# Ahead of the first four pairs of chunks: tiles of x turned as they land, low halves of a chunk in two parts, copies and sums of quanta in another order

## The chip, the cores and the metric

The kernel runs on one core of one Trainium2 chip. The metric is device time in microseconds (us) of one launch, from runs without a profile; the profile is of one further execution. A change of under 0.2% is about what a measurement of this kernel can't tell from none.

## The reference

Two blocks of a transformer in sequence, in float32, for 256 tokens of width 1024. The first block has two layers with adaptive norms over the tokens `x` and a context `ctx` of 256 more; the second has two layers with three attentions each. Only the start of the first layer matters here:

```python
m = jax.nn.silu(cond) @ w_ada + b_ada            # adaln_terms: shift, scale, gate
xl = rms_norm(h_lat, norm_w[li]) * (1.0 + scale_l[:, None, :]) + shift_l[:, None, :]
xc = rms_norm(h_ctx, norm_w[li]) * (1.0 + scale_c) + shift_c
...
au_l, av_l, az_l, bq_l, bk_l, bv_l, bz_l = jnp.split(xl @ w_in, EVEN_SPLITS, axis=-1)
```

Before any product of layer 0 can run, x must be turned so that its columns lie on partitions, its mean squares taken, and the product `silu(cond) @ w_ada` done for the columns concerned. `w_ada` is large: 24 quanta of 256 columns, 1 MB each, are used in the first layers.

## The kernel before

Five engines run hand-written lists of instructions that wait for each other by semaphores; nothing is reordered by a scheduler. Weights come in chunks of 512 KB, numbered r. SyncE (SP) issues their loads into `raw` (four buffers, `load_raw`, L757): the load of chunk r waits until `lo_done` counts r-3, so until chunk r-4 has been split. ScalarE (ACT) copies a chunk into `w_hi` (L839, `split_hi`), VectorE (DVE) writes the rest into `w_lo` (L1341, `split_lo`), and each product is three matmuls: hi x hi, lo x hi, hi x lo (L2088 to L2090).

The start is a pipeline over four pairs. A pair is two of the eight tiles of 128 columns of x, the chunk r = pair of the weights called `av`, and two quanta of `w_ada` (2 x pair and 2 x pair + 1). For each quantum TensorE (PE) multiplies it (`condition`, L2183, banks sc and ac in turn, half by half as the halves land), ACT copies the sum (`ada_evacuate`, L881), PE turns the copy (`condition_turn`, L2199), DVE finishes it (`ada_finish`, L1482 and L1483). With both quanta of a pair done DVE makes the factors (`modulation`, L1488) and the four norm tiles of the pair: `norm_tmp` (L1405) on DVE, `norm_hi` (L854) on ACT, `norm_lo` (L1415) on DVE. Then PE does the pair's products (`value_part`, two tiles e = 0, 1, four groups of 128 tokens n = 0 to 3, three matmuls each).

Ahead of it the four blocks of 128 tokens (two of x, two of ctx, 512 KB each) land in `x_tok`. DVE sums their squares. PE waits for the nine small vectors and for all four blocks, turns the vectors (L2234), and turns x tile by tile (`turn_x`, L2260, four transposes a tile, banks tr in turn), each tile copied into `x_t` by ACT (L860).

After the four pairs come the chunks `au` (r = 4 to 7, slots 4 to 7). Ahead of slot 6 stands `condition_pair(0)` (L2187, its matmuls are L2183 too): the sums of quanta 8 and 9, two halves each. The list of SP that feeds all this is fixed; behind the load of chunk 7 it issues twelve small loads (L788 to L800), then chunk 8, then the four halves of quanta 8 and 9 (L768):

```python
for r in range(HELD, RB + LAYERS_2 * C2):
    load_raw(r)
    ...
    if r - 2 in ADA_OF_SLOT:
        for n in ada_pair(ADA_OF_SLOT[r - 2]):
            load_ada(n)
    if r == 7:
        ...
```

Of the kernel before, what the change touches and what calls it, by code (L numbers as in the profile page):

```python
# [18 lines left out]
F32 = mybir.dt.float32  # L19
F32R = mybir.dt.float32r  # L20
I32 = mybir.dt.int32
ALU = mybir.AluOpType
# [148 lines left out]
NADA = 3 * KT  # L171
ADA_COLS = 256
ADA_FIRST, ADA_ALL, NADA_RAW = 8, 24, 4

# [239 lines left out]
def build_program(nc, t, out):  # L414

    with ExitStack() as ctx:
# [10 lines left out]
        with nc.sbuf_tensor("ada_raw", [P, NADA_RAW, KT, ADA_COLS], F32) as ada_raw:  # L427
# [110 lines left out]
            sem("misc_in"), sem("stored"))  # L538
        rows_in = sem("rows_in")
        ones_set, eps_set, lam_set = sem("ones_set"), sem("eps_set"), sem("lam_set")  # L540
# [100 lines left out]
        def source_at(r):  # L641

            if r >= RB:
# [10 lines left out]
                       (V_QN, t["c_q_norm_w"].rearrange("l (k p) -> (l k) p", p=P)),  # L654
                       (V_KVN, t["c_kv_norm_w"]))

        def ada_bank(n):
# [164 lines left out]
        def _(act):  # L822
# [77 lines left out]

            turned(0, vec[:], tr[:, 0, 0:V_END])
            act.wait_ge(tr_free, 1)
# [3 lines left out]
            def x_turned_to(k):  # L906
                use = TR1_OF[("x", k)]
                turned(use, x_t[:, k, :], tr[:, use % 2, :])

# [4 lines left out]

            for k in range(3):
                x_turned_to(k)
            ada_evacuate(0)
            x_turned_to(3)
            ada_evacuate(1)
            x_turned_to(4)  # L920
            split_hi(0)
            modulated_hi(0, 0)
            x_turned_to(5)
            x_turned_to(6)
            modulated_hi(0, 1)
            x_turned_to(7)
            for pair in range(1, 4):
                ada_evacuate(2 * pair)
                ada_evacuate(2 * pair + 1)
                split_hi(pair)  # L930
                modulated_hi(pair, 0)
                modulated_hi(pair, 1)
            nc.scalar.activation(small[:, 60:61], ones[:, 0:1], ACT.Gelu)
# [392 lines left out]
        def _(dve):  # L1326
# [8 lines left out]
            def split_lo(r):  # L1335
# [6 lines left out]
                last.then_inc(lo_done, 1)  # L1342

            rotations = [0]

# [147 lines left out]
            def modulated_norm(layer, v0, v1, chunk=None):  # L1493
                dve.wait_ge(rs_set, layer + 1)
                for v in range(v0, v1 + 1):
                    u = 2 * KT * layer + v
                    if v < v1:
                        k, half = norm_tile(layer, v)
                        norm_tmp(u, k, (LAT, CTX)[half], amod[:, layer, half, k:k + 1], (LAT, CTX)[half])
                    if chunk is not None and v == v0 + 1:  # L1500
                        split_lo(chunk)
                    if v > v0:
                        k, half = norm_tile(layer, v - 1)
                        norm_lo(u - 1, k, (LAT, CTX)[half], mod[:, layer, k, half:half + 1])

            norm_rsqrt(0, 4)
            for pair in range(4):
                ada_finish(2 * pair)
                if pair:
                    split_lo(pair)  # L1510
                ada_finish(2 * pair + 1)
                dve.wait_ge(ada_set, 2 * pair + 2)
                modulation(0, 2 * pair, 2 * pair + 2, 2 * pair + 2)
                modulated_norm(0, 4 * pair, 4 * pair + 4, chunk=None if pair else 0)
            split_lo(HELD)
# [563 lines left out]
        def _(pe):  # L2079
# [152 lines left out]
            pe.wait_ge(ident_in, 16)  # L2232
            pe.wait_ge(vec_in, 16 * 9)
            nc.tensor.transpose(tr[:, 0, 0:V_END], vec_rows[0:V_END, :], const[0:V_END, K_ID:K_ID + V_END]).then_inc(tr_done, 1)  # L2234
            pe.wait_ge(ones_set, 1)
            for n in range(4):
                pe.wait_ge(x_in[n], 16)
            def value_part(name, j, e, tiles=range(4)):
                c = L0_CHUNKS.index((name, j))
                k, (wh, wl) = 2 * j + e, split_views(c)  # L2240
                if e == 0:
                    pe.wait_ge(lo_done, c + 1)
                for n in tiles:
                    tok = slice(P * n, P * n + P)
                    if name == "av":
                        pe.wait_ge(n_lo, 2 * k + n // 2 + 1)
                    if k == 0 and n == 3:
                        pe.wait_ge(tr_free, TR1_OF[("x" if name == "av" else "ws", KT - 2 if name == "av" else 0)] + 1)
# [13 lines left out]

            turn_x(0)
            turn_x(1)
            turn_x(2)
            pe.wait_ge(cond_set, 1)
            condition(0)
            turn_x(3)
            spread(0, 4)
            condition_turn(0)  # L2270
            condition(1)
            turn_x(4)
            condition_turn(1)
            turn_x(5)
            turn_x(6)
            condition(2)
            turn_x(7)
            for pair in range(4):
                if 0 < pair < 3:
                    condition(2 * pair + 2)  # L2280
                value_part("av", pair, 0, (0, 1))
                if pair < 3:
                    condition_turn(2 * pair + 2)
                    condition(2 * pair + 3)
                value_part("av", pair, 0, (2, 3))
                if pair < 3:
                    condition_turn(2 * pair + 3)
                value_part("av", pair, 1)

# [454 lines left out]
```

## Time and profile before

| | us |
|---|---|
| median of 3 runs (1054.69 to 1056.17) | 1055.52 |
| the profiled execution's own time | 1054.3 |
| its span, first to last instruction | 1052.2 |
| PE busy | 1032.1 (98%) |
| DVE, ACT busy | 733.7, 591.1 |

The span is the profiled execution alone. A busy PE means that a matmul is in flight; the gaps between its groups are what the other engines or a load cost. Times in the views are us from the start of the span.

### The profile page before, as it was taken

The page shows a single profiled execution, that of the slowest core. Times are in us where ns is not written, and L with a number is a line of the kernel's source. Part 1 is how long each engine was busy: PE and PEld are TensorE (multiplying, and loading weights), DVE is VectorE, ACT ScalarE, POOL GpSimd, SP SyncE. Part 2 cuts the span into 40 slices and gives each one's busy share as a digit, 9 for nine tenths or more (in the row PEclk, how much of TensorE's full clock was granted, in tenths as well). Part 3 has the DMA queues.
Part 4 walks back from the last instruction along what each step waited for, and adds up shares of the span by engine and source line. Part 5 has one row for each costly group of instructions (what it writes and reads, how often), then busy time and mean ns, then how long its engine had stood idle before and what let it go on. Part 6 is the DMA issues. An engine that isn't in the chain of part 4 may idle for free.

```text
span 1052.2 us, 17814 instructions
## 1 busy us (share of the span) xinstructions
PE 1032.1 (98%) x6745; PEld 879.4 (84%) x6745; DVE 733.7 (70%) x1569; ACT 591.1 (56%) x1188; POOL 2.6 (0%) x10
## 2 busy tenths in 40 slices
PE   6999999999999999999999999999999999999997
PEld 3677777788986779989898988889989898888886
DVE  4635576786687657797689775658797688665565
ACT  4534245553365556567667664446578767655444
POOL 0000000000000000000000000000000000000000
PEclk9999999999999999999999999999999999999999
DMA  9998661223333225565555556666455456555662
GB/s 328 274 345 264 183 197 41 81 61 100 100 101 91 61 61 151 137 179 141 141 141 160 160 161 193 188 188 182 132 160 161 128 147 166 155 168 179 184 218 81
DMA packets 203693, 165.38 MB, mean 157 GB/s; under 512 B 7117, under 2 KB 172729, under 8 KB 203609
## 3 DMA queue, kind: packets, MB, share of 16 engines
q1 hardware_dynamic: 203088, 163.28, 53.0%
q8 instruction: 54, 0.88, 0.4%
q0 software_dynamic: 192, 0.66, 0.2%
q10 hardware_dynamic: 328, 0.32, 0.1%
q14 instruction: 31, 0.25, 0.1%
HBM read 163.18 MB, written 1.05 MB: 156 GB/s over the span
## 4 chain that ended last, share of the span: by engine, by line
PE 90%; DVE 6%; ACT 2%; issue 1%; DMA 0%; ACTq 0%; DVEq 0%
PE pj L2088 24%; PE pj L2090 23%; PE pj L2089 23%; DVE w_lo L1341 2%; PE tr L2657 1%; PE pj L2183 1%; PE ac L2450 1%; PE tr L2316 1%; PE ac L2593 1%; PE sc L2436 1%; PE sc L2304 1%; PE ac L2330 1%; ACT w_hi L839 1%; PE sc L2439 1%; PE ac L2596 0%
## 5 line engine op out<-in xcount | busy, mean ns | idle before, releaser
L1341 DVE TENSOR_TENSOR w_lo<-raw,w_hi 128x1024 fp32r<-128x1024 f32 (+2 forms) x258 | 309.4, 1202 | 154.5 <-ACT w_hi L839 153.4
L839 ACT ACTIVATE w_hi<-raw 128x1024 fp32r<-128x1024 f32 (+2 forms) x258 | 267.6, 1040 | 97.4 <-PE pj L2090 90.2
L2088 PE MATMUL pj<-h_hi,w_hi 128*128 128x256 f32 (+1 forms) x960 | 297.1, 309 | 0.5 <-DVE m_lo L1747 0.2
L2090 PE MATMUL pj<-h_hi,w_lo 128*128 128x256 f32 (+1 forms) x960 | 290.5, 303 | 0.0
L2089 PE MATMUL pj<-h_lo,w_hi 128*128 128x256 f32 (+1 forms) x960 | 290.3, 302 | 0.0
L2088 PEld LDWEIGHTS pj<-h_hi,w_hi 128*128 128x128 f32 x960 | 183.2, 191 | 16.5 <-issue 8.4
L2090 PEld LDWEIGHTS pj<-h_hi,w_lo 128*128 128x128 f32 x960 | 183.2, 191 | 7.2
L2089 PEld LDWEIGHTS pj<-h_lo,w_hi 128*128 128x128 f32 x960 | 183.4, 191 | 6.3
L2088 PE MATMUL pj<-w_hi,h_hi 128*128 128x512 f32 x344 | 137.3, 399 | 0.4 <-DVE h_lo L1415 0.4
L2090 PE MATMUL pj<-w_hi,h_lo 128*128 128x512 f32 x344 | 134.2, 390 | 0.0
L2089 PE MATMUL pj<-w_lo,h_hi 128*128 128x512 f32 x344 | 134.2, 390 | 0.0
L2088 PEld LDWEIGHTS pj<-w_hi,h_hi 128*128 128x128 f32 x344 | 64.6, 188 | 17.4 <-issue 4.9
L2090 PEld LDWEIGHTS pj<-w_hi,h_lo 128*128 128x128 f32 x344 | 64.6, 188 | 13.9
L2089 PEld LDWEIGHTS pj<-w_lo,h_hi 128*128 128x128 f32 x344 | 64.7, 188 | 12.2
L2088 PE MATMUL pj<-m_hi,w_hi 128*128 128x256 f32 (+1 forms) x160 | 51.5, 322 | 1.1 <-DVE work L1761 0.8
L2090 PE MATMUL pj<-m_hi,w_lo 128*128 128x256 f32 (+1 forms) x160 | 50.4, 315 | 0.0
L2089 PE MATMUL pj<-m_lo,w_hi 128*128 128x256 f32 (+1 forms) x160 | 50.3, 315 | 0.0
L860 ACT ACTIVATE prob_t<-tr 128x512 f32<-128x512 f32 (+2 forms) x56 | 26.2, 518 | 42.6 <-PE tr L2316 40.3
L2088 PE MATMUL pj<-w_hi,m_hi 128*128 128x512 f32 x104 | 40.7, 392 | 0.0
L2090 PE MATMUL pj<-w_hi,m_lo 128*128 128x512 f32 x104 | 40.5, 390 | 0.0
L2089 PE MATMUL pj<-w_lo,m_hi 128*128 128x512 f32 x104 | 40.5, 389 | 0.0
L2088 PEld LDWEIGHTS pj<-m_hi,w_hi 128*128 128x128 f32 x160 | 30.4, 190 | 5.0 <-DVE work L1761 1.7
(376 smaller groups left out, 1479.6 us busy)
## 6 DMA issues: line engine op xcount, KB each, us to landing
raw<-in_w_in_dram SPq DMA_DIRECT2D x152, 512.0 KB, 3.8
ada_raw<-in_ada_w_dram SPq DMA_DIRECT2D x48, 512.0 KB, 8.4
raw<-in_even_w_in_dram SPq DMA_DIRECT2D x28, 512.0 KB, 7.0
raw<-in_w_branch_dram SPq DMA_DIRECT2D x24, 512.0 KB, 3.6
raw<-in_w_out_dram SPq DMA_DIRECT2D x16, 512.0 KB, 4.3
raw<-in_odd_w_in_dram SPq DMA_DIRECT2D x11, 512.0 KB, 4.0
raw<-in_even_w_out_dram SPq DMA_DIRECT2D x8, 512.0 KB, 3.8
raw<-in_odd_w_out_dram SPq DMA_DIRECT2D x8, 512.0 KB, 3.9
```

The costliest lines, as they stand in the source:

```text
L839: last = nc.scalar.activation(hi, src, ACT.Copy)
L860: nc.scalar.activation(dst, src, ACT.Copy).then_inc(tr_free, 1)
L1341: last = nc.vector.tensor_tensor(lo, src, hi.bitcast(F32), ALU.subtract)
L2088: nc.tensor.matmul(dst, lh, rh, start=first, stop=False)
L2089: nc.tensor.matmul(dst, lh, rl, start=False, stop=False)
L2090: return nc.tensor.matmul(dst, ll, rh, start=False, stop=final)
L2183: last = nc.tensor.matmul(sums[32 * c:32 * c + 32, :], cond32[:, 4 * half + c, :], ada_raw[:, n % NADA_RAW, 4 * half + c, :], start=half = ...
L2304: nc.tensor.matmul(sc[:, a, unit_cols(u)], q_e[rows, h, P * i:P * i + P], k_e[rows, h, keys], start=True, stop=True).then_inc(sc_done, 1)
L2316: last = nc.tensor.transpose(tr[:, use % 2, P * j:P * j + P], src[:, P * j:P * j + P], ident)
L2330: last = nc.tensor.matmul(ac[:, P * i:P * i + P], prob_t[:, u % 2, P * j:P * j + P], v_e[:, n, P * h:P * h + P], start=(j == 0), stop=(j = ...
L2436: nc.tensor.matmul(sc[:, e, :], qn_o[:, 2 * hp + e, q], kn_o[:, 2 * hp + e, :], start=True, stop=False)
L2439: last = nc.tensor.matmul(sc[:, e, :], qr_o[rows, hp, q], kr_o[rows, :], start=False, stop=True)
```

## The change

It touches only what stands ahead of and between the first four pairs. PE turns five tiles of x block by block as each block lands (tiles 0 and 1 into tr, tiles 2 to 4 into the three banks pj, `x_bank`), the vectors are turned into ac ahead of the last block, and the tiles 5 to 7 stand between the quanta. `split_lo` of chunks 0 to 3 becomes two halves (`split_lo_half`), behind the second and the fourth `norm_tmp` of the pair; the first half counts `lo_half`, the second `lo_done`. ACT copies the even quantum of the next pair between the pair's norm tiles. PE sums the odd quantum of the next pair two products later, and turns it six matmuls later than before.

```diff
+X_EARLY = 5
...
+        def x_bank(k):
+            return pj[:, k - 2, :] if 2 <= k < X_EARLY else tr[:, TR1_OF[("x", k)] % 2, :]
...
-            for k in range(3):
+            for k in range(4):
                 x_turned_to(k)
             ada_evacuate(0)
-            x_turned_to(3)
+            x_turned_to(4)
+            x_turned_to(5)
             ada_evacuate(1)
-            x_turned_to(4)
             split_hi(0)
+            x_turned_to(6)
             modulated_hi(0, 0)
-            x_turned_to(5)
-            x_turned_to(6)
+            ada_evacuate(2)
             modulated_hi(0, 1)
             x_turned_to(7)
             for pair in range(1, 4):
-                ada_evacuate(2 * pair)
                 ada_evacuate(2 * pair + 1)
                 split_hi(pair)
                 modulated_hi(pair, 0)
+                if pair < 3:
+                    ada_evacuate(2 * pair + 2)
                 modulated_hi(pair, 1)
...
+            def split_lo_half(r, e):
+
+                dve.wait_ge(hi_done, r + 1)
+                part = slice(e * WEL // 2, (e + 1) * WEL // 2)
+                (src, hi, lo), = split_pieces(r)
+                nc.vector.tensor_tensor(lo[:, part], src[:, part], hi[:, part].bitcast(F32), ALU.subtract)\
+                    .then_inc((lo_half, lo_done)[e], 1)
...
-                    if chunk is not None and v == v0 + 1:
-                        split_lo(chunk)
+                    if chunk is not None and v in (v0 + 1, v0 + 3):
+                        split_lo_half(chunk, (v - v0) // 2)
...
                 ada_finish(2 * pair)
-                if pair:
-                    split_lo(pair)
                 ada_finish(2 * pair + 1)
                 dve.wait_ge(ada_set, 2 * pair + 2)
                 modulation(0, 2 * pair, 2 * pair + 2, 2 * pair + 2)
-                modulated_norm(0, 4 * pair, 4 * pair + 4, chunk=None if pair else 0)
+                modulated_norm(0, 4 * pair, 4 * pair + 4, chunk=pair)
...
-            for n in range(4):
-                pe.wait_ge(x_in[n], 16)
+            for i in (0, 2, 1, 3):
+                if i == 3:
+                    pe.wait_ge(vec_in, 16 * 9)
+                    nc.tensor.transpose(ac[:, 0:V_END], vec_rows[0:V_END, :], const[0:V_END, K_ID:K_ID + V_END])\
+                        .then_inc(tr_done, 1)
+                pe.wait_ge(x_in[i], 16)
+                for k in range(X_EARLY):
+                    last = nc.tensor.transpose(x_bank(k)[:, P * i:P * i + P], x_tok[:, i, P * k:P * k + P], ident)
+                    if i == 3:
+                        last.then_inc(tr_done, 1)
...
-            turn_x(0)
-            turn_x(1)
-            turn_x(2)
             pe.wait_ge(cond_set, 1)
             condition(0)
-            turn_x(3)
             spread(0, 4)
             condition_turn(0)
+            turn_x(5)
             condition(1)
-            turn_x(4)
+            turn_x(6)
             condition_turn(1)
-            turn_x(5)
-            turn_x(6)
+            turn_x(7)
             condition(2)
-            turn_x(7)
             for pair in range(4):
-                if 0 < pair < 3:
-                    condition(2 * pair + 2)
                 value_part("av", pair, 0, (0, 1))
                 if pair < 3:
                     condition_turn(2 * pair + 2)
-                    condition(2 * pair + 3)
                 value_part("av", pair, 0, (2, 3))
                 if pair < 3:
+                    condition(2 * pair + 3)
+                value_part("av", pair, 1, (0, 1))
+                if pair < 3:
                     condition_turn(2 * pair + 3)
-                value_part("av", pair, 1)
+                value_part("av", pair, 1, (2, 3))
+                if pair < 2:
+                    condition(2 * pair + 4)
```

DVE's list at the fourth pair (r = 3), before, from the factors' last sum on:

```order
L1341 TENSOR_TENSOR w_lo<-raw,w_hi 128x1024 [waits hi_done]
L1482 TENSOR_REDUCE mod<-ac 128x4 [waits ada_turned]
L1483 TENSOR_TENSOR mod<-mod,vec 128x4 [waits dve_step]
L1488 SCALAR_TENSOR_TENSOR amod<-mod,vec 128x2 [waits ada_set]
L1488 SCALAR_TENSOR_TENSOR amod<-mod,vec 128x2
L1405 SCALAR_TENSOR_TENSOR ntmp<-x_t,amod,sc 128x256 [waits rs_set,amod_set]
L1405 SCALAR_TENSOR_TENSOR ntmp<-x_t,amod,sc 128x256
L1415 SCALAR_TENSOR_TENSOR h_lo<-ntmp,mod,h_hi 128x256 [waits n_hi]
```

The same place with the change:

```order
L1495 TENSOR_REDUCE mod<-ac 128x4 [waits ada_turned]
L1496 TENSOR_TENSOR mod<-mod,vec 128x4 [waits dve_step]
L1501 SCALAR_TENSOR_TENSOR amod<-mod,vec 128x2 [waits ada_set]
L1501 SCALAR_TENSOR_TENSOR amod<-mod,vec 128x2
L1418 SCALAR_TENSOR_TENSOR ntmp<-x_t,amod,sc 128x256 [waits rs_set,amod_set]
L1418 SCALAR_TENSOR_TENSOR ntmp<-x_t,amod,sc 128x256
L1354 TENSOR_TENSOR w_lo<-raw,w_hi 128x512 [waits hi_done]
L1428 SCALAR_TENSOR_TENSOR h_lo<-ntmp,mod,h_hi 128x256 [waits n_hi]
L1418 SCALAR_TENSOR_TENSOR ntmp<-x_t,amod,sc 128x256
L1428 SCALAR_TENSOR_TENSOR h_lo<-ntmp,mod,h_hi 128x256 [waits n_hi]
L1418 SCALAR_TENSOR_TENSOR ntmp<-x_t,amod,sc 128x256
L1354 TENSOR_TENSOR w_lo<-raw,w_hi 128x512 [waits hi_done]
```

The whole low part stood ahead of the odd quantum's finish; now its first half stands between the second `ntmp` and the first `h_lo`, and its second half, the one that counts `lo_done`, behind the fourth `ntmp`.

PE's list from the turn of the last odd quantum (7) to the end of the third pair's products, before:

```order
L2199 MATMUL ac<-const,tanh 128x128 [waits ada_copied]
L2199 MATMUL ac<-const,tanh 128x128
L2088 MATMUL pj<-w_hi,h_hi 128x512 [waits n_lo]
L2089 MATMUL pj<-w_lo,h_hi 128x512
L2090 MATMUL pj<-w_hi,h_lo 128x512
L2088 MATMUL pj<-w_hi,h_hi 128x512 [waits n_lo]
L2089 MATMUL pj<-w_lo,h_hi 128x512
L2090 MATMUL pj<-w_hi,h_lo 128x512
L2088 MATMUL pj<-w_hi,h_hi 128x512 [waits n_lo]
L2089 MATMUL pj<-w_lo,h_hi 128x512
L2090 MATMUL pj<-w_hi,h_lo 128x512
L2088 MATMUL tr<-w_hi,h_hi 128x512 [waits n_lo]
```

With the change, from the same turn on, into the fourth pair's first product:

```order
L2210 MATMUL ac<-const,tanh 128x128 [waits ada_copied]
L2210 MATMUL ac<-const,tanh 128x128
L2099 MATMUL pj<-w_hi,h_hi 128x512 [waits n_lo,lo_done]
L2100 MATMUL pj<-w_lo,h_hi 128x512
L2101 MATMUL pj<-w_hi,h_lo 128x512
L2099 MATMUL tr<-w_hi,h_hi 128x512 [waits n_lo]
L2100 MATMUL tr<-w_lo,h_hi 128x512
L2101 MATMUL tr<-w_hi,h_lo 128x512
L2099 MATMUL pj<-w_hi,h_hi 128x512 [waits n_lo,lo_half]
```

Twelve matmuls stood between the turn and the next pair's first product, now six. In the earlier pairs the sum of the next even quantum follows them, before and after.

## Rows read from the trace of the kernel before

**Rows 1.** The page: busy time, share of the span, instructions.
```profile
PE 1032.1 (98%) x6745; PEld 879.4 (84%) x6745; DVE 733.7 (70%) x1569; ACT 591.1 (56%) x1188; POOL 2.6 (0%) x10
```

**Rows 2.** Who waited for whom, 0 to 47 us, PE: in total, times, longest.
```profile
PE tr L2234 <- DMA scr<-in_c_kv_norm_w_dram: 8.9, 1, 8.9
PE sc L2199 <- ACT tanh L881: 0.8, 1, 0.8
PE sc L2183 <- DMA ada_raw<-in_ada_w_dram: 0.5, 1, 0.5
PE pj L2088 <- DVE h_lo L1415: 0.4, 1, 0.4
```

**Rows 3.** Timeline of PE: start, us, what, [idle before it and its releaser].
```profile
9.29 2.96 PE L2260 MATMUL tr<-const,work 128*128 128x128 f32 x12
12.17 1.68 PE L2183 MATMUL sc<-ada_raw,cond 128*32 128x256 f32 x16
...
15.49 1.07 PE L2183 MATMUL ac<-ada_raw,cond 128*32 128x256 f32 x16
...
19.57 0.64 PE L2183 MATMUL sc<-ada_raw,cond 128*32 128x256 f32 x8 [0.51 <-DMA ada_raw<-in_ada_w_dram]
...
20.76 0.47 PE L2088 MATMUL pj<-w_hi,h_hi 128*128 128x512 f32 x1
...
31.59 0.38 PE L2199 MATMUL sc<-const,tanh 128*128 128x128 f32 x2
31.90 1.07 PE L2183 MATMUL ac<-ada_raw,cond 128*32 128x256 f32 x16
...
46.34 0.47 PE L2088 MATMUL pj<-w_hi,h_hi 128*128 128x512 f32 x1 [0.44 <-DVE h_lo L1415]
```

**Rows 4.** Timeline of DVE, the fourth pair.
```profile
42.78 1.23 DVE L1341 TENSOR_TENSOR w_lo<-raw,w_hi 128x1024 fp32r<-128x1024 f32 x1 [2.02 <-ACT w_hi L839]
43.92 0.17 DVE L1482 TENSOR_REDUCE mod<-ac 128x4 f32<-128x16 f32 x1
...
44.59 0.87 DVE L1405 SCALAR_TENSOR_TENSOR ntmp<-x_t,amod,sc 128x256 f32<-128x256 f32 x2
45.71 0.49 DVE L1415 SCALAR_TENSOR_TENSOR h_lo<-ntmp,mod,h_hi 128x256 fp32r<-128x256 f32 x1 [0.25 <-ACT h_hi L854]
46.11 0.48 DVE L1405 SCALAR_TENSOR_TENSOR ntmp<-x_t,amod,sc 128x256 f32<-128x256 f32 x1
...
50.42 1.23 DVE L1341 TENSOR_TENSOR w_lo<-raw,w_hi 128x1024 fp32r<-128x1024 f32 x1 [1.98 <-ACT w_hi L839]
```

**Rows 5.** Timeline of SP: issue of each load, time the issue took.
```profile
44.03 0.37 SPq L757 DMA_DIRECT2D raw<-in_even_w_in_dram  x1
44.44 0.58 SPq L788 DMA_DIRECT2D const<-in_consts_dram  x1
...
50.28 0.61 SPq L800 DMA_DIRECT2D prob<-in_a_ws_dram  x1
51.67 0.38 SPq L757 DMA_DIRECT2D raw<-in_even_w_in_dram  x1
```

**Rows 6.** Who waited for whom, 43 to 53 us, SP's queue.
```profile
SPq L757 <- DVE w_lo L1341: 4.9, 2, 4.1
```

**Rows 7.** Instructions on ada_raw, window at 55.2 us: the last two halves of quanta 8, 9.
```profile
L768 SPq DMA_DIRECT2D ada_raw<-in_ada_w_dram x2: 756/806/857, 54.3 to 55.1; - x2
...
DMA to landing us min/median/max: 8.1/8.4/8.8
```

**Rows 8.** Timeline of PE, 62.5 to 65 us.
```profile
62.91 1.93 PE L2183 MATMUL pj<-ada_raw,cond 128*32 128x256 f32 x32
64.77 0.50 PE L2088 MATMUL pj<-h_hi,w_hi 128*128 128x512 f32 x1
```

**Rows 9.** Stretches: PE, PEld, DVE, ACT, POOL busy (count), PEclk, DMA share, GB/s.
```profile
43.00:45.00 2.00, 2.00 (x11) 1.66 (x10) 1.90 (x7) 0.00 (x0) 0.00 (x0) 1.00 0.17 47
...
49.00:53.00 4.00, 4.00 (x19) 3.31 (x18) 1.23 (x1) 3.83 (x8) 0.00 (x0) 1.00 0.55 180
53.00:64.00 11.00, 11.00 (x65) 8.59 (x67) 6.66 (x11) 3.75 (x5) 0.00 (x0) 1.00 1.08 344
```

More of the change, by code:

```diff
@@ L538, in build_program @@
             sem("misc_in"), sem("stored"))
-        rows_in = sem("rows_in")
+        rows_in, lo_half = sem("rows_in"), sem("lo_half")
         ones_set, eps_set, lam_set = sem("ones_set"), sem("eps_set"), sem("lam_set")
@@ L899, in _ @@
                 nc.scalar.dma_start(vec_rows[c0:c0 + src.shape[0], :], src).then_inc(vec_in, 16)
-            turned(0, vec[:], tr[:, 0, 0:V_END])
+            turned(0, vec[:], ac[:, 0:V_END])
             act.wait_ge(tr_free, 1)
@@ L907, in x_turned_to @@
                 use = TR1_OF[("x", k)]
-                turned(use, x_t[:, k, :], tr[:, use % 2, :])
+                turned(use, x_t[:, k, :], x_bank(k))
             def value_evacuate(name, n):
@@ L2232, in _ @@
             pe.wait_ge(ident_in, 16)
-            pe.wait_ge(vec_in, 16 * 9)
-            nc.tensor.transpose(tr[:, 0, 0:V_END], vec_rows[0:V_END, :], const[0:V_END, K_ID:K_ID + V_END]).then_inc(tr_done, 1)
+            for i in (0, 2, 1, 3):
[8 more added lines that the diff above has]
+                        last.then_inc(tr_done, 1)
             pe.wait_ge(ones_set, 1)
-            for n in range(4):
-                pe.wait_ge(x_in[n], 16)
             def value_part(name, j, e, tiles=range(4)):
@@ L2240, in value_part @@
                 k, (wh, wl) = 2 * j + e, split_views(c)
-                if e == 0:
+                if e == 0 and name == "av":
+                    pe.wait_ge(lo_half, j + 1)
+                else:
                     pe.wait_ge(lo_done, c + 1)
@@ L2246, in value_part @@
                         pe.wait_ge(n_lo, 2 * k + n // 2 + 1)
+                    if name == "av" and k == 0 and n == 0:
+                        pe.wait_ge(tr_free, TR1_OF[("x", X_EARLY - 1)] + 1)
                     if k == 0 and n == 3:
```

## The prediction

> **What bounds the kernel now.** I read the busy times first: PE is in flight for 1032.1 us of a span of 1052.2 [rows 1], so the end moves only with what PE waits for, and with what its first matmul waits for. The list of PE's waits says how little that is in the first 47 us: the first turn, 0.8 for ACT's copy of quantum 2, 0.5 for a load, 0.4 for the fourth pair's `h_lo` [rows 2]. Between 47 and 300 us the same view is empty. So the change can win 0.8 + 0.4 us of waits and some of the start, and it can lose wherever PE's next supplier has little in hand. The timelines of PE, DVE and SP were read for that, in this order, and then one landing time: that of the last half of quanta 8 and 9, which `condition_pair(0)` takes at slot 6, ten us behind the edited stage.
>
> **Part 1, x turned as it lands.** The first product stands at 20.76. Ahead of it PE sums quantum 2, whose last half began only at 19.57, released by its load after 0.51 of waiting [rows 3]. No load of the start moves. With the change nothing stands between that sum and the first product, so the product comes at 19.57 + 0.6 = 20.2: -0.55. The rest of the transposes' time is not won; the loads hide it.
>
> **Part 2, ACT's copies in another order.** The copy of quantum 2 stands ahead of the second half of the norm tiles and no longer behind the last x tile. PE's wait of 0.76 for it goes: -0.75.
>
> **Part 3, the turn of the odd quantum later, half a low part in the chain.** From the start of that turn to the next pair's first product: turn 0.38 [rows 3], DVE's start 0.05, sum and factors 0.67 (43.92 to 44.59), two `ntmp` 0.79, the first half of the low part, `h_lo` to PE 0.63 (45.71 to 46.34) [rows 3, 4]. The half has no row. The whole, 1024 columns, takes 1.14 of the engine (42.78 to 43.92), a 256-column step 0.40 (45.71 to 46.11) [rows 4]; those are the bounds, and I take 0.6, between them by columns. Sum 3.1. What PE has to do meanwhile: turn 0.14, six matmuls at 0.23 with 0.2 of changeover, and the next even sum of 1.0 (31.90 to 32.90 in [rows 3], where the next group follows): 2.7. So PE waits 0.4 ahead of the second and of the third pair. Ahead of the fourth no sum follows: 3.1 - 1.7 = 1.4 to 1.5, where it was 0.44. Together +0.4 +0.4 +1.05 = +1.85. (If the half cost 1.14 it would be +3.5; if 0.4, +1.25.)
>
> The stage by itself: -0.55 - 0.75 + 1.85 = **+0.55**, next to nothing. The fourth pair's first product comes at about 46.9 and not 46.34.
>
> **Part 4, `lo_done` of chunk 3, and what SP has queued behind it.** This decides. The low part of chunk 3 now ends at 42.78 + 1.23 = 44.01 and SP issues chunk 7 at 44.03 [rows 4, 5]; the view of SP's waits shows that wait, 4.1 us, on `w_lo` [rows 6]. With the change `lo_done` is counted by the second half, behind four `ntmp` and two `h_lo`. Back from 46.9: the first `ntmp` starts at 46.9 - 0.63 - 0.6 - 0.79 = 44.9. Forward: 0.79 + 0.6, then two `h_lo` and two `ntmp` at 0.40, then 0.7 for the half: 48.6. I take 4.5 later, since one or two tenths of the waits are mine by rounding.
>
> Behind chunk 7 SP issues twelve small loads one by one, from 44.44 to 50.28 + 0.61 = 50.9, then chunk 8 at 51.67 [rows 5]. That is 6.9 us from chunk 7's issue with no wait in it; the second wait of [rows 6], 0.8, is for chunk 4's low part, ended 50.42 + 1.23 = 51.65 [rows 4]. With the change the twelve end at 48.5 + 6.9 = 55.4, chunk 4 is split by then, and chunk 8 goes at 55.4: +3.75. The four halves of quanta 8 and 9 follow. The last is issued at 55.1 and lands 8.8 later, at 63.9 [rows 7]. PE's 32 matmuls on them start at 62.91, the next group at 64.77, so the last quarter starts at 62.91 + 3/4 x 1.86 = 64.3 [rows 8]: **0.4 us in hand**. From 53 us on the DMA share is 1.08 and moves 344 GB/s, against 0.55 in 49 to 53 [rows 9]. So these loads are bound by bytes behind a start that SP sets. The landing moves by 3.75 at least if the queue fills the idle share that chunk 8 leaves today, by 4.5 if it all slides along; I take 4.1, near the middle, as the queue is half idle just there.
>
> PE then stands in `condition_pair(0)` until 63.9 + 4.1 + its last quarter. What PE won or lost before is swallowed: the total is 4.1 - 0.4 = **+3.7**. Behind it the waits list is empty to 300 us, so nothing gives it back; loads and users slide together.
>
> **Sum.** 1054.3 + 3.7 = 1058.0 for a profiled execution. The median of the runs shown stands 1.2 above the profiled one, so 1055.5 + 3.7 = **1059.2**.
>
> **The clock, against the skill.** The sum of quantum 0 took 1.68, that of quantum 1 1.07 [rows 3]: the first ran at the lower of the two levels for most of its length, after twelve transposes that had kept PE at work from 9.29 on [rows 3]. The Trainium skill (TensorE: Matmul & The Clock Gate, Part 4: PE-mode transpose) says that transposes don't count as activity for the clock gate. The trace agrees. By that rule the twenty early transposes don't lift the clock, and my sum, which takes the first sums as they are, would be late by the third rival's amount.
>
> **Rivals.**
> *Not slower.* The landing of quantum 9 doesn't slide by more than 0.95 (0.4 in hand plus the 0.55 by which PE comes later). For it: the DMA is 0.17 busy in 43 to 45 and 0.55 in 49 to 53 [rows 9], so a late list could be caught up if the transfers, and not SP, made its length. Against it: SP's 6.9 us are issue times, one behind the other. It decides at `lo_done` of chunk 3: before about 45 it is true. The time would be the stage's alone, from -1.3 (no new waits) to +0.55: 1054.2 to 1056.1. Chance 0.16.
> *The clock falls in the new wait.* PE would work 0.4 us, wait 1.1, three times over. The granted clock is 1.00 in all stretches read [rows 9], and none has such a wait, so the trace can't exclude it. Price: at the start the lower level held from 8.9 to somewhere in the first sum, about 4.5 us, of which half is lost, 2.2: 1059.2 + 2.2 = 1061.4. The skill's page (TensorE: Matmul & The Clock Gate, Part 1) has the lower level as the default that activity lifts; no row here shows a fall. Chance 0.08.
> *The clock rises later at the start.* The sum of quantum 0 is cut in two by its load, so the rise could slip behind the sums of quanta 0 and 1. Each costs 0.6 more at the lower level (1.68 - 1.07), part of it under loads: 0.9 on the stage, on `lo_done` and so on the end: 1060.1. Chance 0.10.
>
> **Numbers.** About 2.1 us (0.2%) is what a measurement can tell from no change. My forecast, +3.7, has 0.66; its own bounds are a landing 3.0 later (stage without waits, queue caught up) and 5.0 later: 1058.2 to 1060.2, with half a us for the median of three runs. Slower by over 0.2%: the forecast and both clock rivals, 0.84, less 0.02 for the low edge: 0.82. The first rival gives mostly no difference, 0.14, and faster 0.04, for which its 1.3 us would not even do. The range 1057.2 to 1061.3 leaves out that rival and part of the falling clock.
>
> **What would show it.** Right: first product near 20.2; waits of 0.4 before the pairs two and three, 1.4 before the fourth; SP issues chunk 7 near 48.5 and chunk 8 near 55.4; PE's waits list gains "pj L2194 <- DMA ada_raw" of 3 to 4 us, in pieces of about 1, at 63 to 68. Wrong: chunk 7 issued before 45; no wait on ada_raw at slot 6; a fourth pair that starts a us earlier than 46.3; a granted clock under 1.00 behind 63 us.

## The result, and the profile after

The changed kernel takes **1062.66 us** (median of 4, 1062.19 to 1064.04) against 1055.7 (median of 4) for the kernel before on the same chip: ratio **1.0069**, 95% interval [1.0052, 1.0087], +7.0 us. The forecast was 1059.2, in a range to 1061.3: slower, as foretold, but by nearly twice as much. The profiled execution, the slowest of the four, took 1064.04 us with a span of 1061.9 (before 1054.3 and 1052.2), +9.7, so what its trace shows adds up to more than the +7.0 of the medians.

PE's waits in the first 90 us, who waited for whom, in total, times, longest (before: [rows 2]):

```profile
PE tr L2251 <- DMA work<-in_x_dram: 5.7, 2, 5.3
PE pj L2194 <- DMA ada_raw<-in_ada_w_dram: 3.0, 4, 0.9
PE pj L2099 <- DVE h_lo L1428: 2.1, 3, 1.4
PE pj L2099 <- DVE w_lo L1354: 1.0, 1, 1.0
PE sc L2194 <- DMA ada_raw<-in_ada_w_dram: 0.6, 1, 0.6
PE sc L2194 <- DVE cond L1474: 0.6, 1, 0.6
PE sc L2238 <- DVE col L1375: 0.3, 1, 0.3
```

The second line is the one that the forecast named, with its 3.0 us in four pieces. Waits cover less than the loss, though. Where the rest is, the timeline of PE shows; first the start and the pairs (before: [rows 3]):

```profile
10.19 0.65 PE L2251 MATMUL pj<-const,work 128*128 128x128 f32 x3
11.44 0.64 PE L2194 MATMUL sc<-ada_raw,cond 128*32 128x256 f32 x8 [0.61 <-DVE cond L1474]
12.71 0.64 PE L2194 MATMUL sc<-ada_raw,cond 128*32 128x256 f32 x8 [0.62 <-DMA ada_raw<-in_ada_w_dram]
13.64 1.86 PE L2238 MATMUL sc<-const,col 128*128 128x128 f32 x8 [0.30 <-DVE col L1375]
...
19.38 1.34 PE L2194 MATMUL sc<-ada_raw,cond 128*32 128x256 f32 x16
21.70 0.47 PE L2099 MATMUL pj<-w_hi,h_hi 128*128 128x512 f32 x1 [0.97 <-DVE w_lo L1354]
...
30.46 0.47 PE L2099 MATMUL pj<-w_hi,h_hi 128*128 128x512 f32 x1 [0.35 <-DVE h_lo L1428]
...
39.24 0.47 PE L2099 MATMUL pj<-w_hi,h_hi 128*128 128x512 f32 x1 [0.35 <-DVE h_lo L1428]
...
47.99 0.47 PE L2099 MATMUL pj<-w_hi,h_hi 128*128 128x512 f32 x1 [1.35 <-DVE h_lo L1428]
```

The waits at the pairs are the forecast's. But the first product is at 21.70, not 20.2. The spread (L2238) took 1.86 where it took 1.06 before: PE ran at the lower clock level. The stretches give it (columns as in [rows 9]):

```profile
14.00:17.00 3.00, 3.00 (x18) 2.59 (x20) 0.34 (x2) 0.46 (x2) 0.00 (x0) 0.50 1.08 366
...
62.00:68.00 6.00, 3.92 (x28) 2.21 (x26) 3.12 (x9) 0.60 (x1) 0.00 (x0) 1.00 1.09 353
68.00:72.00 4.00, 3.13 (x19) 1.26 (x20) 0.00 (x0) 0.96 (x2) 0.00 (x0) 0.57 1.07 373
72.00:76.00 4.00, 4.00 (x12) 3.14 (x11) 1.23 (x1) 0.58 (x1) 0.00 (x0) 0.58 1.10 349
...
437.00:440.00 3.00, 3.00 (x17) 3.00 (x16) 2.67 (x11) 0.00 (x0) 0.00 (x0) 0.53 0.00 0
```

The granted clock falls from 2.4 to 1.2 GHz three times: near 14, at 68.5 for 6.8 us, and near 437 for 3.4. Before, it rose at 13.5, in the first sum, and stayed up until the last 5 us.

The middle fall stands in the new waits. DVE's fourth pair, SP's list behind it, and PE at `condition_pair(0)` (before: [rows 4, 5, 8]):

```profile
45.97 0.87 DVE L1418 SCALAR_TENSOR_TENSOR ntmp<-x_t,amod,sc 128x256 f32<-128x256 f32 x2
46.76 0.69 DVE L1354 TENSOR_TENSOR w_lo<-raw,w_hi 128x512 fp32r<-128x512 f32 x1
...
48.94 0.69 DVE L1354 TENSOR_TENSOR w_lo<-raw,w_hi 128x512 fp32r<-128x512 f32 x1
```

```profile
49.65 0.37 SPq L761 DMA_DIRECT2D raw<-in_even_w_in_dram  x1
50.06 0.58 SPq L792 DMA_DIRECT2D const<-in_consts_dram  x1
...
55.89 0.61 SPq L804 DMA_DIRECT2D prob<-in_a_ws_dram  x1
56.55 0.58 SPq L761 DMA_DIRECT2D raw<-in_even_w_in_dram  x1
57.17 4.72 SPq L772 DMA_DIRECT2D ada_raw<-in_ada_w_dram  x4
```

```profile
65.48 0.64 PE L2194 MATMUL pj<-ada_raw,cond 128*32 128x256 f32 x8 [0.84 <-DMA ada_raw<-in_ada_w_dram]
66.90 0.64 PE L2194 MATMUL pj<-ada_raw,cond 128*32 128x256 f32 x8 [0.79 <-DMA ada_raw<-in_ada_w_dram]
68.41 1.03 PE L2194 MATMUL pj<-ada_raw,cond 128*32 128x256 f32 x8 [0.87 <-DMA ada_raw<-in_ada_w_dram]
69.90 1.08 PE L2194 MATMUL pj<-ada_raw,cond 128*32 128x256 f32 x8 [0.46 <-DMA ada_raw<-in_ada_w_dram]
70.91 0.80 PE L2099 MATMUL pj<-h_hi,w_hi 128*128 128x512 f32 x1
```

`lo_done` of chunk 3 comes at 49.6 (44.0 before), chunk 7 is issued then, the twelve small loads take 6.9 us, chunk 8 goes at 56.55 (51.67). Eight matmuls of a half take 0.64 in the first two, 1.08 in the last: the clock fell at the start of the third, after PE had waited 0.84, 0.79 and 0.87 with 0.6 us of work between.

To place the loss, each `ACTIVATE` of ACT was set beside the same one of the kernel before, counted from the end (both have 1031): how much later it starts, by where it stood before. The shift is a staircase, flat but for two stretches:

| at, before | 54 | 147 | 425 | 468 | 979 |
|---|---|---|---|---|---|
| changed kernel | +1.6 | +8.3 | +8.3 | +9.8 | +9.7 |

So all of it arises before 147 us, but for 1.5 us at the fall near 430. The experiments are read by the same table.

### The profile page after: what moved, and what is told of

It is laid out like the page before. It is cut to its first block, busy times and chain, and to the rows that moved or that the text cites. A ratio compares the mean times of both kernels' runs of the same rounds, so it can differ in the third digit from the quotient of the medians.

```text
span 1061.9 us, 17824 instructions
## 1 busy us (share of the span) xinstructions
PE 1039.2 (98%) x6745; PEld 883.4 (83%) x6745; DVE 733.1 (69%) x1573; ACT 592.0 (56%) x1188; POOL 2.6 (0%) x10
## 4 chain that ended last, share of the span: by engine, by line
PE 88%; DVE 6%; issue 2%; DMA 1%; ACT 1%; SPq 1%; DVEq 0%; ACTq 0%
PE pj L2099 23%; PE pj L2101 22%; PE pj L2100 22%; DVE w_lo L1346 2%; PE tr L2675 1%; PE ac L2468 1%; PE pj L2194 1%; PE tr L2334 1%; PE ac L2611 1%; PE sc L2454 1%; PE sc L2322 1%; PE ac L2348 1%; ACT w_hi L843 1%; DMA ada_raw<-in_ada_w_dram 1%; PE sc L2457 1%
## 5 line engine op out<-in xcount | busy, mean ns | idle before, releaser
L1346 DVE TENSOR_TENSOR w_lo<-raw,w_hi 128x1024 fp32r<-128x1024 f32 (+2 forms) x254 | 304.6, 1202 | 152.6 <-ACT w_hi L843 151.4
L2101 PEld LDWEIGHTS pj<-w_hi,h_lo 128*128 128x128 f32 x344 | 64.6, 188 | 13.9
```

Of the source, the lines that this page charges most:

```text
L1346: last = nc.vector.tensor_tensor(lo, src, hi.bitcast(F32), ALU.subtract)
L2101: return nc.tensor.matmul(dst, ll, rh, start=False, stop=final)
```

## The experiments

The kernel before, run again beside the experiments, took 1054.96, 1055.18 and 1055.09; each ratio below is against the one run on the same chip. The theory: SP's list, delayed by chunk 3's second low half, sets the time. The rivals: the changed start, the later turns, the clock.

**sp_16 and sp_13: the kernel before, with nothing late but SP.** (`n_lo` counts the finished `h_lo` tiles.)

```diff
                 if r >= NRAW:
                     sp.wait_ge(lo_done, r - NRAW + 1)
+                if r == 7:
+                    sp.wait_ge(n_lo, 16)      # sp_13: 13
```

> The kernel before, with one added wait of SP ahead of the load of chunk 7: until the last norm tile of the fourth pair is finished (n_lo 16), which the trace of before has at 48.4 us. Nothing else is changed. If SP's list behind chunk 7 is what makes the change slow, this alone costs most of it: chunk 7 issued at 48.5 (44.03 before), the last half of quantum 9 landing 20 us behind it at 68.6, 4.3 us later for PE than the 64.3 at which it takes it, in waits of about 1 us on ada_raw. If the fall of the clock in those waits is part of the cost, 2.2 us more: +6.5 in all, near 1062; without it +4.3. If instead the order of the pairs' steps makes the change slow, this is 0.

> As the run before, with the wait on n_lo 13, about 46.3 us. SP's list: chunk 7 at 46.3, quantum 9 complete at 66.3, +2.0 us, in waits of about half a us that should leave the clock up: 1057.7. If a small delay is caught up by transfers that pack more densely, 0 to 1. If the clock falls here too, +4.

Measured: sp_16 **1062.43** (1061.82 to 1063.14), ratio 1.007 [1.0055, 1.0085]; sp_13 **1058.21** (1055.77 to 1060.4), 1.0028 [1.0017, 1.0038]. Chunk 7 was issued at 48.33 and 46.74. With TensorE, ACT and DVE as before, SP's delay alone makes the whole slowdown. In sp_16 PE, which is not late here, waits longer:

```profile
65.33 0.64 PE L2185 MATMUL pj<-ada_raw,cond 128*32 128x256 f32 x8 [2.56 <-DMA ada_raw<-in_ada_w_dram]
```

and its clock falls at 67.0, behind this wait and one of 0.78. In sp_13's trace it doesn't fall there: two waits, of 0.49 and 0.86, and +2.3 at 147.

**small_first: the changed kernel, the twelve small loads one place earlier.** They then go while chunk 7 waits.

```diff
-                if r == 7:
+                if r == 6:
                     sp.dma_start(const[:, 0:K_PRC], ...
```

> The changed kernel with the twelve small loads issued behind chunk 6 and not behind chunk 7. SP's list: they go out at 41 to 48, while SP waits for chunk 3's low part; chunk 8 follows chunk 4's low part at 53.3, quantum 9 is complete before 63.5, PE doesn't wait in condition_pair(0) and the clock stays up there. What is left is the stage's own shift, 47.99 against 46.34: +1.65 against before, 1057.3, 5 to 5.5 under the changed kernel. If the pairs' order were the cause, it stays near 1062.

Measured: **1056.17** (1054.68 to 1057.6), ratio 1.0014 [1.0005, 1.0023]. By the ratios nearly 6 of the 7 us are gone. The stage's waits are all still there (0.15, 0.35, 1.36 at the pairs), and at 147 the shift is +0.2: in this execution the stage itself is worth next to nothing, and SP's list nearly all. The 1.5 us on top of it in this trace come at the fall near 430.

```profile
28.95 0.47 PE L2099 MATMUL pj<-w_hi,h_hi 128*128 128x512 f32 x1 [0.15 <-DVE h_lo L1428]
...
63.05 1.93 PE L2194 MATMUL pj<-ada_raw,cond 128*32 128x256 f32 x32
64.91 0.50 PE L2099 MATMUL pj<-h_hi,w_hi 128*128 128x512 f32 x1
```

**small_before: the same move in the kernel before.**

(`if r == 7` becomes `if r == 6`, nothing else.)

> The kernel before with the twelve small loads one place earlier in SP's list, nothing else changed. They go into the time in which chunk 7 waits for chunk 3's low part, so they cost nothing and give nothing, since no wait stands at condition_pair(0) in the kernel before: 1054.5 to 1055.5. If the earlier place by itself were worth time, and the result of small_first were due to that rather than to a delay taken away: under 1053.5.

Measured: 1054.76 (1053.63 to 1055.46), 0.9993 [0.9984, 1.0001]. No difference: small_first gives time back, and the place itself gives none.

**filled: work in the waits of `condition_pair(0)`.**

```diff
+                    for _ in range(4):
+                        nc.tensor.matmul(tr[:, 0, :], h_hi[:, 0, 0:P], h_hi[:, 0, :], start=True, stop=True)
                     pe.wait_ge(ada_in[half][n % NADA_RAW], 16 * (n // NADA_RAW + 1))
```

> The changed kernel with four matmuls of 512 columns into a bank that nobody reads ahead of each of the four halves in condition_pair(0), 0.9 us of work in waits of 0.8, so that PE has no idle time there. They leave the output as it is. If the fall of the clock from 68.5 to 75.3 is owed to PE's idle time, the clock stays at 1.00 and the time is 2 us under the changed kernel, 1060.5. If it falls anyway, or its cost was hidden, no difference (or 0.3 more for the added matmuls).

Measured: **1060.87** (1060.69 to 1061.67), 1.0058 [1.0041, 1.0075]: by the medians 1.8 us less than the changed kernel and by the ratios 1.1, with intervals that overlap, though PE does 16 matmuls more that nobody reads. In its trace the clock stays up:

```profile
68.00:72.00 4.00, 4.00 (x28) 2.15 (x27) 0.00 (x0) 0.77 (x2) 0.00 (x0) 1.00 1.07 373
```

The medians alone don't give the price of the fall, as filled's trace has no fall near 430 either. The traces give it: in filled the shift stays as it is behind `condition_pair(0)` (+6.3 at the next group, +6.4 at 147), in pairs_only (below) it grows there from +4.9 to +7.0. So the clock's fall costs 2.1 us and comes on top of the late loads. That filled stands at +6.3 so early is another matter: SP took 5.41 us for its four ada loads (4.36 in pairs_only) and issued the last at 61.0 (59.9).

**start_only and pairs_only: the change in two halves.** start_only has the early turning, and ACT's and TensorE's lists as in the change up to the first product but for ACT's copy of quantum 2, which stands where it stood before, and the pairs of before; pairs_only has the opposite. The lines that differ most:

```diff
 # start_only, against the changed kernel
-                if e == 0 and name == "av":
-                    pe.wait_ge(lo_half, j + 1)
-                else:
+                if e == 0:
                     pe.wait_ge(lo_done, c + 1)
...
-                modulated_norm(0, 4 * pair, 4 * pair + 4, chunk=pair)
+                modulated_norm(0, 4 * pair, 4 * pair + 4, chunk=None if pair else 0)
```

> The changed start alone (tiles of x turned as they land, ACT's copies there), with the four pairs as they were before. If the delay comes from chunk 3's second low half reaching SP's list late, this kernel has none of it: chunk 7 issued at about 44, quantum 9's last half at about 64, no wait at condition_pair(0), and a time of 1054.5 to 1055.5 where the clock stays up at the start. The first product should then start at 20.2 to 20.4 (20.1 in the changed kernel with the small loads first). Rival: the clock falls at 14 in most executions with this start; then the first product starts at 21.7 and the time is 1056.0 to 1056.5. If the start alone were the cause of the delay: over 1059.

> The changed pairs alone (the odd turn one product group later, halves of the low part, ACT's copies there) behind the start of before. If SP's list is the cause: waits of 0.35, 0.35 and 1.35 at the pairs' starts, chunk 7 issued at about 48.7, chunk 8 at about 55.6, quantum 9's last half landed at about 68.5 to 69, waits of 0.5 to 0.9 at each half of condition_pair(0) and the clock down there: 1061 to 1062.5. If the changed start were needed for the delay (its clock fall, the later products): 1057 or less.

Measured: start_only 1056.63 (1054.43 to 1057.2), 1.0009 [1.0, 1.0018]; pairs_only **1062.64** (1061.66 to 1063.23), 1.0068 [1.0055, 1.0081]. The pairs alone give the result. In pairs_only the start is as before, so it measures the forecast's fourth part undisturbed:

```profile
48.84 0.37 SPq L757 DMA_DIRECT2D raw<-in_even_w_in_dram  x1
...
55.73 0.58 SPq L757 DMA_DIRECT2D raw<-in_even_w_in_dram  x1
56.35 4.36 SPq L768 DMA_DIRECT2D ada_raw<-in_ada_w_dram  x4
```

```profile
68.66 1.08 PE L2191 MATMUL pj<-ada_raw,cond 128*32 128x256 f32 x8 [0.41 <-DMA ada_raw<-in_ada_w_dram]
69.67 0.80 PE L2096 MATMUL pj<-h_hi,w_hi 128*128 128x512 f32 x1
```

start_only gains nothing by its early turns: PE waits 0.84 and 0.78 for the halves of quantum 2, which land when they land, and the first product is at 20.74 (before 20.76).

**odd_early and whole_3: which edit in the pairs makes the low part late.** odd_early puts TensorE's and ACT's order in the pairs back and keeps the halves:

```diff
                 value_part("av", pair, 0, (0, 1))
                 if pair < 3:
                     condition_turn(2 * pair + 2)
+                    condition(2 * pair + 3)
                 value_part("av", pair, 0, (2, 3))
                 if pair < 3:
-                    condition(2 * pair + 3)
-                value_part("av", pair, 1, (0, 1))
...
```

whole_3 writes both halves of chunk 3 in a row:

```diff
-                    if chunk is not None and v in (v0 + 1, v0 + 3):
+                    if chunk is not None and v == v0 + 1 and chunk == 3:
+                        split_lo_half(chunk, 0)
+                        split_lo_half(chunk, 1)
+                    elif chunk is not None and v in (v0 + 1, v0 + 3) and chunk < 3:
                         split_lo_half(chunk, (v - v0) // 2)
```

> The changed kernel with TensorE's and ACT's order in the pairs as before (the odd quantum's turn ahead of the first products' second half), and the low part of a chunk still in two parts within the chain. The chain then starts 1.4 us earlier at each pair and carries 0.6 us more than before: a wait of about 1.0 at the fourth pair and none at the others. Chunk 3's second low half ends at about 47.3, chunk 7 is issued there, between the two delays already measured (46.74 cost 2.3 us at 147, 48.33 cost 7.4): 3 to 4 us at 147, and with the 1.5 us of the fall near 430 a time of 1058 to 1059.5. If the late turn alone, not the halves, were what makes the low part late: 1056 or less.

> The changed kernel with both halves of chunk 3's low part in a row, behind the first ntmp of the fourth pair, instead of around the next two. It is ready at 48.0 instead of 49.6, so chunk 7 and all behind it on SP's list come 1.6 us earlier, and the fourth pair's h_lo comes 0.6 later, which the products before it do not hide (wait of 1.9 to 2.0 instead of 1.35). By SP's list the time falls by 1.6, to 1061.0; if the clock no longer falls in the waits of condition_pair(0), by 3.6, to 1059. If the waits at the pairs' starts set the time: 0.6 more than the changed kernel, 1063.2.

Measured: odd_early 1060.48 (1059.1 to 1062.75), 1.0054 [1.004, 1.0068]; whole_3 **1058.18** (1056.91 to 1060.61), 1.0033 [1.002, 1.0047]. Chunk 7 at 46.45 and 46.87. Counted from the first product, chunk 7 goes 23.3 us later in the kernel before (44.03 less 20.76), 26.3 in odd_early (46.45 less 20.19), 28.0 in pairs_only (48.84 less 20.87) and 27.9 in the changed kernel. So the halves make 3.0 of the delay, and the late turns with ACT's order 1.7 (the two were put back together). odd_early missed its expectation by 1 us, and whole_3 came out 0.8 under the better of its two figures, with a first product at 20.46. The pair tells why: odd_early issues earlier and ends later. Its PE is early at `condition_pair(0)` (61.4) and waits four times; its clock falls at 64.1, behind the first two waits (1.09 and 0.78). In whole_3 PE, held up by 1.96 at the fourth pair, arrives at 63.9, finds two halves there and waits twice; the clock stays up from its rise to the last microseconds:

```profile
63.91 1.07 PE L2197 MATMUL pj<-ada_raw,cond 128*32 128x256 f32 x16
65.77 0.64 PE L2197 MATMUL pj<-ada_raw,cond 128*32 128x256 f32 x8 [0.79 <-DMA ada_raw<-in_ada_w_dram]
67.27 0.64 PE L2197 MATMUL pj<-ada_raw,cond 128*32 128x256 f32 x8 [0.86 <-DMA ada_raw<-in_ada_w_dram]
```

Of whole_3's five runs two took 1060.5 and 1060.6, as long as odd_early's median, so the two medians are less sure than the two traces (+3.1 and +4.6 at 147).

**start_filled and thin_filled: the two other falls.** Both start from small_first. start_filled puts eight plain products of 128 columns (two matmuls each in the views) into the waits around quantum 0's sums; thin_filled puts 3 + 3 products of 256 columns around the sixteen one-column products of layer 2's sums of squares, behind which the fall near 430 begins:

```diff
 # start_filled: ahead of quantum 0's sum and between its halves; 2 behind it
+            def fill(count):
+
+                for _ in range(count):
+                    nc.tensor.matmul(sc[:, 0, 0:P], ident, x_tok[:, 0, 0:P], start=True, stop=True)
+
+            fill(3)
             pe.wait_ge(cond_set, 1)
-            condition(0)
+            condition(0, lambda: fill(3))
+            fill(2)
...
 # thin_filled: ahead of and inside sum_squares
+                for _ in range(3 if s == 2 else 0):
+                    nc.tensor.matmul(tr[:, 1, 0:256], h_hi[:, 0, 0:P], h_hi[:, 0, 0:256], start=True, stop=True)
```

> The changed kernel with the small loads first, and eight plain products of 128 columns whose sums nobody reads, put into the waits before, inside and behind quantum 0's sums (10.9 to 13.9). If the spread of small_first (1054.7 to 1057.6) comes from the clock's fall at 14, which these waits leave room for: the clock stays up there in every run, the first product starts at 20.1 to 20.5, the time is 1054.8 to 1055.3 and its runs lie within 1 us but for the fall near 437. If the fall at the start costs nothing: 1056.2 as in small_first, or 0.2 to 0.5 more for the added products.

> The changed kernel with the small loads first, and three products of 256 columns ahead of and three between the sixteen products of one column at 426 to 428 (the sums of squares of layer 2), whose results nobody reads. If the last 1.5 us in the changed kernel's trace, which small_first and start_only show alone, are the clock's fall behind these thin products: no fall near 430 in any run, the granted clock at 0.998 or more in all, and 1055.0 + 0.7 for the added products, with a spread of runs under 1.5 us. If the fall does not hang on them: 1056.2 + 0.7 = 1056.9, with the same spread as small_first.

Measured: start_filled 1055.95 (1054.34 to 1057.67), 1.0008 [0.9999, 1.0017]: no better than small_first, and the runs still 3 us apart. Its expectation failed. Its profiled run is its slowest; its clock has no fall near 14 but rises only at 13.6, so the first three added products ran at the lower level (1.49 us for their six matmuls) and held up the sums behind them:

```profile
11.05 1.49 PE L2289 MATMUL sc<-work,const 128*128 128x128 f32 x6
12.47 1.08 PE L2196 MATMUL sc<-ada_raw,cond 128*32 128x256 f32 x8
...
21.85 0.47 PE L2099 MATMUL pj<-w_hi,h_hi 128*128 128x512 f32 x1 [0.88 <-DVE w_lo L1354]
```

This trace also qualifies small_first's: the stage is 1.8 us late at 54, nothing waits at `condition_pair(0)` to swallow it, and +2.0 is left at 147. So with SP's list out of the way the stage's own lateness counts, +0.2 or +2.0 as the start goes.

thin_filled 1055.51 (1054.94 to 1058.26), 1.0008 [0.9999, 1.0016]. Its trace has no fall near 430 and a step of +0.7 there (small_first +1.5), which is the six added products' own time at 0.12. But filled, whole_3, small_before and the kernel before show no fall either, without such products, and 4 of its 11 runs have a clock of 0.997 or less. It agrees with the theory of the thin products and doesn't settle it.

All traces in one table (us). The third column is the issue of the first half of quantum 8, the first of the four loads that `condition_pair(0)` needs:

| kernel | chunk 7 issued | quantum 8 issued | shift at 147 | 468 less 425 | clock at `condition_pair(0)` | median (ratio) |
|---|---|---|---|---|---|---|
| before | 44.03 | 52.10 | 0 | 0 | up | 1055.2 |
| small_before | 48.97 | 52.50 | +0.5 | 0.0 | up | 1054.76 (0.9993) |
| start_only | 44.02 | 52.09 | 0.0 | +1.5 | up | 1056.63 (1.0009) |
| small_first | 48.19 | 52.45 | +0.2 | +1.5 | up | 1056.17 (1.0014) |
| thin_filled | 48.50 | 53.10 | +0.5 | +0.7 | up | 1055.51 (1.0008) |
| start_filled | 49.83 | 54.37 | +2.0 | +1.5 | up | 1055.95 (1.0008) |
| sp_13 | 46.74 | 54.27 | +2.3 | +1.5 | up | 1058.21 (1.0028) |
| whole_3 | 46.87 | 54.39 | +3.1 | 0.0 | up | 1058.18 (1.0033) |
| odd_early | 46.45 | 53.98 | +4.6 | +1.5 | falls | 1060.48 (1.0054) |
| sp_16 | 48.33 | 56.23 | +7.4 | +1.5 | falls | 1062.43 (1.0070) |
| filled | 48.91 | 56.43 | +6.4 | 0.0 | up | 1060.87 (1.0058) |
| pairs_only | 48.84 | 56.35 | +7.0 | +1.5 | falls | 1062.64 (1.0068) |
| changed | 49.65 | 57.17 | +8.3 | +1.5 | falls | 1062.66 (1.0069) |

A late chunk 7 alone costs nothing: small_before issues it at 48.97 and takes no longer. What costs is the lateness of the four loads behind chunk 8.

No version beats the kernel before: the best, small_before, is the same.

## Why the prediction was right in kind and short in size

The path was the one foreseen: `lo_done` of chunk 3, SP's list, PE at `condition_pair(0)`. The step that failed is the sum at the end of Part 4, 4.1 - 0.4 = +3.7. It took the slide of the landing as 4.1, and in pairs_only it was 4.8; and it held nothing for the clock, whose fall in the new waits stood beside it as a rival of 0.08 and cost 2.1 there.

**Part 1 (first product 20.2, -0.55): wrong in the changed kernel's trace, and not worth its name elsewhere.** In that trace the clock fell at 13.9, the spread (1.86) and the sum of quantum 1 (1.34 for 1.07) ran slower, and the product, held by the first low half of chunk 0, came at 21.70. In small_first, with the clock up, it came at 20.14, as forecast; in start_only at 20.74. The step missed that all depends on the landing of quantum 2's last half, which differs between executions by as much as the term (the sum of that half starts at 19.57 in small_first, 20.18 in start_only, 20.35 in filled).

**Part 2 (-0.75): right.** The wait for ACT's copy of quantum 2 is in no list of waits of a kernel with ACT's new order; in start_only, where the copy is behind the last tile again, it is back with 0.7.

**Part 3 (waits of 0.4, 0.4 and 1.4 to 1.5; half a low part 0.6): right.** 0.35, 0.35, 1.35; the halves take 0.60 of the engine (46.76 to 47.36). The bounds of the half, 0.4 and 1.14, were not needed. The 32.90 at which the forecast's even sum ends is so in the trace, though [rows 3] doesn't show it.

**Part 4 (+3.7), the step that carried the forecast: right as mechanism, under-sized.** In pairs_only `lo_done` comes 4.8 later (forecast 4.5), the small loads take 6.9 (6.9), chunk 8 goes 4.06 later (3.75). From there to the last half of quantum 9 it was 3.4 us of issuing before (51.67 to 55.1), now 4.2 (55.73 to 59.9), landing 8.8 later again. So the landing moved by 4.8 and not by 4.1. I had bounded it by 4.5, "if it all slides along"; the list did more than slide, as four ada loads took SP 4.36 instead of 3.88, and chunk 8 ahead of them 0.58 instead of 0.38. Before, the line was:

```profile
52.10 3.88 SPq L768 DMA_DIRECT2D ada_raw<-in_ada_w_dram  x4
```

With 0.4 in hand, and the last eight matmuls 0.4 longer at the lower clock, PE's next group stands at 69.67 instead of 64.77: +4.9.

**The rival "The clock falls in the new wait": it came true, and belonged in the sum.** I gave it 0.08 as an alternative to the forecast. It isn't one: in every trace in which PE waited for all four halves with nothing in between, the clock fell. The price, 2.2, was right: in pairs_only the shift goes from +4.9 at 64.77 to +7.0 at 147, 2.1 us. That the two agree so well is in part luck, as the 2.2 was taken from the start, where the lower level had held for 4.5 us, and here it held for 6.8. Of my reason, "none has such a wait, so the trace can't exclude it", the second half should have led to a larger chance. The Trainium skill (TensorE: Matmul & The Clock Gate, Part 1, A second HAM failure mode) describes a clock that swings where PE idles shortly and often between groups of matmuls, in a kernel that cycles through PSUM banks. The trace agrees in that short waits were enough: 0.84, 0.79, 0.87 with 0.6 of work between, then half the clock; here they are waits for loads, and it is a single fall.

**The third rival, "The clock rises later at the start": not in the changed kernel's trace, where it rose earlier.** It rested on the rule that transposes don't lift the clock, with "The trace agrees" behind it. It doesn't. In whole_3 PE did nothing but transposes until 11.24, and three of them took 0.85 us at 7.04 and 0.55 at 8.66: the clock rose at 8.8, 4.7 us earlier than in the kernel before.

```profile
7.04 0.85 PE L2254 MATMUL pj<-const,work 128*128 128x128 f32 x3
8.18 0.69 PE L2254 MATMUL tr<-const,work 128*128 128x128 f32 x2 [0.29 <-DMA work<-in_x_dram]
8.66 0.55 PE L2254 MATMUL pj<-const,work 128*128 128x128 f32 x3
```

It rose at 10.5 in the changed kernel, and fell back at 13.9 in the waits of 0.61, 0.62 and 0.30; whole_3 had the same three waits, of 0.93, 0.63 and 0.30, and no fall. In the kernel before the rise comes at 13.5, in the sum behind the twelve transposes; that fits both readings, so its trace could not decide. The moment differs between executions of the same start: in thin_filled, with the same early transposes as whole_3, it came only at 14.7, and its first product at 20.54, so the rival's lateness exists too, at 0.4 against small_first's 20.14. The rule itself (TensorE: Matmul & The Clock Gate, Part 4: PE-mode transpose) is not borne out here.

**The sum of pairs_only, profiled:** 4.9 to the next group, 2.1 of slow clock behind it, 1.5 at the fall near 430: 8.5 on 1054.3, the 1062.80 of that run. The forecast had 3.7 of it. Missed: 1.2 in the slide and the last sums, 2.1 and 1.5 of clock. The last, 1.5, no rival had. It is not in every execution: the profiled run has a mean granted clock of 0.993, the other four of pairs_only 0.996, too high for both falls, 10.2 us at half in 1061. Without it 4.9 + 2.1 = 7.0 stands against the 7.2 us of its ratio, 1.0068. In the changed kernel's own trace the stage is 0.8 later than in pairs_only (47.99 against 47.18, the fall near 14), and the last half's sum 1.2 later (69.90 against 68.66). So what PE loses in the stage is not swallowed, as the forecast had it: it makes `lo_done` and SP's list later as well.

**The rival "Not slower": false**, by its own mark, chunk 3's low part before 45. small_first shows that it would have come near had SP's list been ready: +0.2 at 147 with all the new waits of the stage in place.

**"Nothing gives it back"** was right: the shift stays within 0.1 from 468 to the end.

Open: why the fall near 430 shows in the traces of most kernels with a changed start or a delay and not in the kernel before; the one attempt at it, thin_filled, leaves it at an agreement. Also, why the four ada loads take SP longer to issue behind a late chunk 8.

## What to carry to other kernels

When an edit moves a semaphore that a load queue waits on, add up everything that is queued behind that wait, small loads included, and compare it with the slack of the last consumer; here 0.4 us of slack stood against 4 us, and moving twelve small loads ahead of the wait gave most of the 7 us back (1.0069 to 1.0014). If the answer is that the TensorE will wait for pieces that land one by one, price the clock with it: the waits and the fall are one case and not two. And being late can be free where the engine would have to wait anyway: of odd_early and whole_3, which issued chunk 7 at 46.45 and 46.87, the one that held PE up at the fourth pair stood 1.5 us better at 147. That is one trace of each; their runs overlap.

## What the runs showed of the hardware

- The granted clock fell to half behind two or three short waits of PE, with sums of 0.6 us between them: 0.84, 0.79 and 0.87 (changed kernel, at 68.5), 1.09 and 0.78 (odd_early, at 64.1), 0.46, 0.78 and 0.87 (pairs_only, at 67.1), 2.56 and 0.78 (sp_16, at 67.0). It stayed up with 0.79 and 0.86 (whole_3) and with 0.49 and 0.86 (sp_13), where two halves in one piece, 1.07 us of work, stood ahead of them. At the start it fell with waits of 0.61, 0.62 and 0.30 (changed kernel) and not with 0.93, 0.63 and 0.30 (whole_3). So the length of the waits alone doesn't tell.
- Once fallen it stayed down for 6.8 us at `condition_pair(0)`, in four traces, though PE was fully busy from 70.9 on in the changed kernel; near 14 and near 430 for 3.4 us.
- The clock rose while PE had done nothing but transposes, at 8.8, 9.5 and 10.5 us (whole_3, odd_early, changed kernel) and, with the start of before, at 12.4 and 13.1 (sp_16, small_before). In thin_filled it rose only at 14.7.
- Added work is no safe way to raise the clock: at the lower level it takes longer and stands ahead of the sums (start_filled: three products in 1.49 us at 11.05, three more in 0.98 at 13.48, where the clock rose).
